# Block two's output projection done one token tile at a time, with the norms and transposes of a tile placed beside the next tile's products; the last norm by tile, too

## The reference, cut to what matters

```python
mix = jnp.concatenate([ya, yb, yc, yd], axis=-1).astype(dt)
x = x + rms_norm(mix @ w_out[l], norm_mix_post[l])
h = rms_norm(x, norm_mlp_pre[l])
ff = jnp.square(jax.nn.relu(h @ mlp_w1[l])) @ mlp_w2[l]
x = x + rms_norm(ff, norm_mlp_post[l])
```

## Time and profile before

| what | us |
|---|---|
| median of three runs (lowest, highest) | 2509.2 (2503.89, 2513.76) |
| the profiled execution: its own time | 2511.92 |
| its span in the trace | 2510.1 |
| mean granted TensorE clock over the span | 0.913 of 2.4 GHz |
| TensorE busy, share of the span | 2115.8, 84% |
| VectorE busy, share | 637.0, 25% |
| ScalarE busy, share | 325.3, 13% |

### The profile page before, as it was taken

The page is one execution under the profiler, slowest core; times in us unless marked ns, Lnnn a source line. Parts: engine busy times, 40 slices in busy tenths (PEclk is TensorE's granted clock), DMA queues, the critical chain, the costliest instruction groups (busy, mean ns, idle before and its releaser), DMA issues. The chain is left out here.

```text
span 2510.1 us, 41882 instructions
## 1 busy us (share of the span) xinstructions
PE 2115.8 (84%) x17677; PEld 1018.7 (41%) x17677; DVE 637.0 (25%) x1155; ACT 325.3 (13%) x627; POOL 253.8 (10%) x299
## 2 busy tenths in 40 slices
PE   6992469369988999999989983499988959999997
PEld 4541353324432444444334431245676324444443
DVE  2005632411211121121111213566564030000001
ACT  2002200200100111011001100143233010000000
POOL 1104500211000100100100102001210000000000
PEclk9996659579998999999999997799997979999998
DMA  9533001679999999999999999100100052211000
GB/s 369 207 128 122 3 0 34 257 307 380 397 419 419 418 418 419 410 418 418 419 419 415 418 419 358 35 34 1 47 11 35 9 201 80 88 67 75 34 0 34
DMA packets 131455, 548.47 MB, mean 219 GB/s; under 512 B 19546, under 2 KB 32878, under 8 KB 81938
## 3 DMA queue, kind: packets, MB, share of 16 engines
q1 hardware_dynamic: 105360, 506.21, 50.1%
q0 software_dynamic: 9264, 27.04, 2.8%
q10 hardware_dynamic: 16690, 13.06, 1.6%
HBM read 523.54 MB, written 22.71 MB: 218 GB/s over the span
## 5 line engine op out<-in xcount | busy, mean ns | idle before, releaser
L1250 PE MATMUL ps<-W,x_turned 128*32 128x512 f32 x3168 | 371.9, 607 | 27.3 <-DMA W<-in_w_gu 16.0
L1250 PE MATMUL ps<-W_high,x_turned 128*32 128x512 f32 x2016 | 236.4, 605 | 22.5 <-DMA W_high<-in_w_gu 16.5
L1346 DVE TENSOR_SCALAR gate<-ps 128x256 f32<-128x256 f32 x81 | 34.4, 425 | 816.7 <-PE ps L1255 816.7
L2584 PE MATMUL ps<-hT,W 128*128 128x512 f32 x512 | 224.5, 599 | 8.3 <-PEq L1450 6.3
L2622 PE MATMUL ps<-W,hid 128*128 128x512 f32 x512 | 221.6, 593 | 2.7 <-PEq L2566 1.7
L1250 PEld LDWEIGHTS ps<-W,x_turned 128*32 128x32 f32 x3168 | 97.7, 111 | 231.6 <-issue 191.7
L1268 PE MATMUL ps<-W,hidden_turned 128*32 128x256 f32 x3200 | 185.1, 384 | 2.5 <-ACT hidden_turned L1300 2.5
L2584 PEld LDWEIGHTS ps<-hT,W 128*128 128x128 f32 x512 | 97.7, 192 | 134.5 <-issue 134.5
L2622 PEld LDWEIGHTS ps<-W,hid 128*128 128x128 f32 x512 | 96.6, 190 | 127.7 <-issue 127.7
L1655 PE MATMUL ps<-hT,W 128*128 128x512 f32 x336 | 146.5, 594 | 1.7 <-PEq L1450 1.4
L1268 PEld LDWEIGHTS ps<-W,hidden_turned 128*32 128x32 f32 x3200 | 104.5, 112 | 87.4 <-issue 20.9
(11 more groups left out here) (541 smaller groups left out, 2083.2 us busy)
## 6 DMA issues: line engine op xcount, KB each, us to landing
W<-in_w_gu SPq DMA_DIRECT2D x152, 1024.0 KB
W_high<-in_w_gu SPq DMA_DIRECT2D x104, 1024.0 KB
W<-in_w_down SPq DMA_DIRECT2D x80, 1024.0 KB
W_high<-in_w_down SPq DMA_DIRECT2D x48, 1024.0 KB
W<-in_mlp_w SPq DMA_DIRECT2D x16, 2048.0 KB, 8.1
W<-in_w_ada SPq DMA_DIRECT2D x12, 2048.0 KB, 16.3
W<-in_w_in SPq DMA_DIRECT2D x10, 2048.0 KB, 16.1
moe_y<-y_rows ACTq DMA_DIRECT2D x324, 32.0 KB
```

The costliest lines, as they stand in the source:

```text
L1250: last = pe.matmul(gu_bank[SUB * j:SUB * (j + 1), :].rearrange("p (s n) -> p s n", s=2), xs[:, kk % 2, kk // 2, :], ex.view(n)[:, :, j * 2 ...
L1346: dve.tensor_scalar(gate[:], gu_bank[:, 0:256], SWIGLU_LIMIT, None, ALU.min).then_inc(gated, 1)
L2584: last = pe.matmul(ps[j % 8][:], w.tile(n)[:, kk, (j % 4) * P:(j % 4 + 1) * P], hT[:, kk, :], start=kk == 0, stop=kk == KD - 1)
```

## The change

The projection now loops over token tiles outside and column halves inside. Behind each tile's second half stand, on ScalarE and VectorE, that tile's post norm, residual add, pre norm, scaling (into `b_r` and `b_k`, memory of the mixer that is free by then, in turn) and, after its transposes, the move into `hT`. On TensorE the transposes of tile i - 1 stand behind the products of tile i. The block of `phase_norm_turn` for the MLP is gone, and so is one block end. SyncE issues the MLP's weight loads in the projection's block; the fifth and sixth go to the two slots that hold `w_out`, and wait until those are used. The banks of a tile's products are used again for its transposes. In the last phase the norm goes tile by tile too, and `out` is stored in eight pieces of 256 KB where there were four of 512 KB. Root and mean are made with one VectorE instruction fewer (the 1/D goes into the root's scale).

```diff
-class post_norm:
+class PostNorm:
...
+    def scalar(self, act, i, mm):
+        for s in range(2):
+            act.wait_ge(mm, 2 * i + s + 1)
+            act.activation(self.junk, self.k.ps[2 * i + s][:], ACT.Square, accum_out=self.ms[:, i, s:s + 1]).then_inc(self.sq, 1)
+            act.wait_ge(self.sq, 2 * i + s + 1)
+        act.wait_ge(self.summed, i + 1)
+        act.activation(self.rt[:, i:i + 1], self.rt[:, i:i + 1], ACT.Sqrt, scale=1.0 / D).then_inc(self.sd, 1)
+
+    def vector(self, dve, i):
+        dve.wait_ge(self.sq, 2 * i + 2)
+        dve.tensor_scalar(self.rt[:, i:i + 1], self.ms[:, i, 0:1], self.ms[:, i, 1:2], D * EPS, ALU.add, ALU.add).then_inc(self.summed, 1)
+        dve.wait_ge(self.sd, i + 1)
+        dve.reciprocal(self.rt[:, i:i + 1], self.rt[:, i:i + 1]).then_inc(self.vch, 1)
...
+        for s in range(2):
...
+            dve.scalar_tensor_tensor(out=self.tmp[:, s, :], in0=self.k.ps[2 * i + s][:], scalar=self.rt[:, i:i + 1], in1=self.w[:, s, :], op0=ALU.mult, op1=ALU.mult).then_inc(self.vch, 1)
+        for s in range(2):
...
+            dve.tensor_tensor(self.k.h[:, i, cols], self.k.h[:, i, cols], self.tmp[:, s, :], ALU.add).then_inc(self.done, 1)
...
+def phase_out_2(nc, k, a, w, mixT, hT, room):
...
+        @block.sync
+        def _(sp):
+            post.sync(sp)
+            w.load(sp, w.first["mlp1"], w.first["mlp1"] + SLOTS)
...
+            def turn(i):
+                for s in range(2):
+                    pe.wait_ge(xnd, 2 * i + s + 1)
+                    for q in range(4):
+                        last = pe.transpose(ps[2 * i + s][:, q * P:(q + 1) * P], xn[i % 2][:, (4 * s + q) * P:(4 * s + q + 1) * P], k.ident[:])
+                    last.then_inc(tr, 1)
+
+            for i in range(TT):
+                for half in range(2):
...
+                    for kk in range(KD):
+                        last = pe.matmul(ps[2 * i + half][:], mixT[:, kk, i * P:(i + 1) * P], w.tile(O2 + half)[:, kk, :], start=kk == 0, stop=kk == KD - 1)
+                    last.then_inc(mm, 1)
...
+                if i:
+                    turn(i - 1)
+            turn(TT - 1)
...
+        @block.vector
+        def _(dve):
+            for i in range(TT):
+                post.vector(dve, i)
+                dve.wait_ge(hsq, 2 * i + 2)
...
+                for s in range(2):
...
+                    dve.tensor_scalar(xn[i % 2][:, s * 512:(s + 1) * 512], k.h[:, i, s * 512:(s + 1) * 512], rt[:, i:i + 1], None, ALU.mult).then_inc(xnd, 1)
+                for s in range(2):
+                    dve.wait_ge(tr, 2 * i + s + 1)
...
+                    dve.tensor_tensor(hT[:, 4 * s:4 * s + 4, i * P:(i + 1) * P], ps[2 * i + s][:].rearrange("p (q t) -> p q t", q=4), gain, ALU.mult).then_inc(ev, 1)
...
@@ phase_mlp_down
-                sp.wait_ge(post.done, 2 * i + 2)
-                sp.dma_start(out[0, i * P:(i + 1) * P, :], k.h[:, i, :]).then_inc(out_done, 16)
...
+                for s in range(2):
+                    sp.wait_ge(post.done, 2 * i + s + 1)
+                    sp.dma_start(out[0, i * P:(i + 1) * P, s * 512:(s + 1) * 512], k.h[:, i, s * 512:(s + 1) * 512]).then_inc(out_done, 16)
...
@@ second_block
-            phase_norm_turn(nc, k, "_mlp", VEC["norm_mlp_pre_2"], hT, room, lambda sp: w.load(sp, w.first["mlp1"], w.first["mlp1"] + SLOTS))
```

More of the change, by code:

```diff
@@ L2492, in _, with __init__ @@
             dve.wait_ge(hfin, 2)
[L2495 to L2518, removed]
-class post_norm:
-    def __init__(self, nc, k, st, tag, wrow):
+class PostNorm:
+    def __init__(self, nc, k, st, tag, wrow, room=None):
         sem = lambda n: k.semaphore(n + tag)
@@ L2527, in __init__ @@
         self.k, self.wrow = k, wrow
[L2528 to L2532, removed]
-    def sync(self, sp):
-        sp.dma_start(self.w[:], self.wrow.rearrange("(o d) -> o d", o=1).to_broadcast([P, D])).then_inc(self.w_in, 16)
@@ L2537, in scalar @@
[L2537 to L2559, removed]
@@ new lines, in __init__ @@
+        if room is None:
+            room = sb("post_room", [P, 5, 512])[:]
+        self.w = room[:, 0:2, :]
+        self.tmp = room[:, 2:4, :]
+        self.junk = room[:, 4, :]
+        self.ms, self.rt = sb("post_ms", [P, TT, 2]), sb("post_rt", [P, TT])
+        self.w_in, self.sq, self.vch, self.summed, self.sd, self.done = (sem(n) for n in ("post_w_in", "post_sq", "post_vch", "post_sum", "post_sd", "post_done"))
+    def sync(self, sp):
+        sp.dma_start(self.w.rearrange("p a b -> p (a b)"), self.wrow.rearrange("(o d) -> o d", o=1).to_broadcast([P, D])).then_inc(self.w_in, 16)
@@ L2602, in _, with phase_mlp_down @@
                 dve.tensor_tensor(hid[:, j, :], tmp[:, j % 2, :], tmp[:, j % 2, :], ALU.mult).then_inc(sqd, 1)
-def phase_mlp_down(nc, k, a, w, hid, out):
+def phase_mlp_down(nc, k, a, w, hid, out, room):
     ps = k.ps
@@ L2610, in phase_mlp_down @@
         sem = lambda n: k.semaphore(n)
-        mm, out_done = sem("down_mm"), sem("out_done")
-        post = post_norm(nc, k, st, "_mlp", a["norm_mlp_post_2"][0])
+        mm, used, out_done = sem("down_mm"), sem("down_used"), sem("out_done")
+        post = PostNorm(nc, k, st, "_mlp", a["norm_mlp_post_2"][0], room)
         block = st.enter_context(nc.Block())
@@ L2626, in _ @@
                 if g < 7:
-                    last.then_inc(mm, 1)
-                    pe.wait_ge(mm, g + 1)
+                    last.then_inc(used, 1)
+                    pe.wait_ge(used, g + 1)
                     pe.sem_inc(w.used, 1)
@@ new lines, in _ @@
+                for s in range(2):
+                    sp.wait_ge(post.done, 2 * i + s + 1)
+                    sp.dma_start(out[0, i * P:(i + 1) * P, s * 512:(s + 1) * 512], k.h[:, i, s * 512:(s + 1) * 512]).then_inc(out_done, 16)
+            sp.wait_ge(out_done, 32 * TT)
+        @block.scalar
+        def _(act):
+            for i in range(TT):
+                post.scalar(act, i, mm)
+        @block.vector
+        def _(dve):
+            for i in range(TT):
+                post.vector(dve, i)
+            dve.wait_ge(post.done, 2 * TT)
@@ L2664, in second_block @@
             phase_mlp_up(nc, k, a, w, hT, hid)
-        phase_mlp_down(nc, k, a, w, hid, out)
+            phase_mlp_down(nc, k, a, w, hid, out, hT[:, 0:5, :])
 def build(nc, inputs):
```

77 lines of the change are left out of this document (56 added, 21 removed).

## The result

The changed kernel took 2480.75 us in the median of four runs (2477.0 to 2482.86), the kernel before beside it 2509.71 (2503.89 to 2513.76). The ratio is 0.9881, with a 95% interval of 0.9861 to 0.9901: between 25 and 35 us faster. The profiled execution has a span of 2479.2 us where before it was 2510.1.

A forecast was written before the change was run, and what follows sets the result against it. TensorE bounds the whole span but idles in two gaps, where the change can gain: 20.5 us at the projection plus 9.1 at the end, 29.6 off the 2509.2 median, gives 2479.6 us, range 2472 to 2487.

The forecast's parts named there:

- the early issues lose their cover: Gap before the MLP: if SyncE's weight issues were no longer hidden beside the products, 4.4 us would come back.
- (a): Gap after the last square: tile 2's transposes and two moves into hT keep VectorE busy until 2.3 us.
- (b): Last tile's list, from the sum to the scale: 0.98 less 0.19 for the dropped instruction, 0.79 us.
- (c): Last tile's two scales and two adds on VectorE: 0.65 three times and 0.69 for the last, ending at 5.7 us.
- (e): Last tile's pre norm: 0.79 us again to the scaling, 0.35 for its first half plus 0.1; TensorE starts at 7.7.
- (d): ScalarE's square of the second half, 0.72 us to VectorE's sum; the first half's square hidden behind the second add.
- (g): Block's end to the MLP's first instruction: 0.5 us, bringing the gap to 11.0, with SyncE no longer late.
- Beside the products: Two groups of eight transposes moved among the projection's products: 1.0 us each plus 0.1 of start, 2.2 lost.
- The end: Last square to the end of the span: 6.8 us against 15.9, a gain of 9.1 (8.7 to 9.8).
- the warm rival: Clock stays up through the gap: last transposes cost 0.8 us less, the MLP's start 2.8 less; 2476.0, chance 0.10.
- The slow rival: Tile lists on VectorE and ScalarE outlast a 13.9 us product group, stalling TensorE twice; 2519 at 25 us, chance 0.02.
- That the late weight loads hold the block's end: Before the MLP: two late loads hold the block's end and the last list isn't short; 2497, chance 0.05.

The follow-up runs named there:

- e1: Kernel before with four of the first six MLP weight loads issued in the projection's block: 2502.61 us, ratio 0.9966.
- e3: Changed kernel with all six MLP weight loads held until the projection's products are done: 2490.21 us, ratio 0.9907.
- e9: Kernel before with four MLP weight loads issued early and the changed kernel's last phase (norm by tile, eight stores): 2491.48 us, ratio 0.9931.
- e11: Changed kernel run once more with no edit, beside two others on one chip: 2480.31 us, ratio 0.9876.
- e5: Changed kernel with sixteen added VectorE instructions in the lists of token tiles 0 to 2, ahead of the scaling: 2491.19 us, ratio 0.9931.
- e6: Changed kernel with the MLP's first eight products done early, on token tiles 0 to 2, in the last tile's wait: 2473.06 us, ratio 0.9847.

## Why the prediction was right

It said 2479.6 and came out at 2480.75, inside 2472 to 2487, and the terms behind it hold one by one, save that of the clock in the MLP. By the ruler the gain is 2.3 above the 29.6 of the sum: 0.3 in the gap, 0.4 beside the products, 0.2 at the end and 1.3 in the MLP.

- **What bounds the gap.** Right, and shown by e1 and e3: the serial norms, and SyncE's issues. The prediction put the latter at 4.4 us; it measured 4.56 (e9 against the kernel before), or 4.8 in e1. Too small was its 4.4 for the case that the early issues lose their cover: with all six behind the products, e3 lost 9.6, as the short list covers less of the 20 us that they take.
- **(a) Tile 2's transposes and moves ahead of the list: 2.3.** Measured 1.93 (2012.33 to 2014.26). The new form of the move, a tensor-tensor with a repeated gain, took 0.69 and a pitch of 0.6, at the lower bound of 0.6.
- **(b) 0.79, (c) 2.6, (e) first half 0.79.** Measured 0.73, 2.60 and 0.74.
- **(d) The second square: 0.72.** Measured 0.95. The first half's square is not hidden as cleanly as assumed: with its read of the sum it runs to 0.2 behind the last add, where the second begins.
- **(e) to (g).** Scaling to transposes 0.54 (0.45), transposes and moves 2.70 (2.8), block's end 0.52 (0.5). Sum 10.71, predicted 11.0, with misses of at most 0.4 in single terms that partly cancel.
- **Beside the products: 2.2.** Measured 1.76. The second trace, e11, seems to say 0.4, but its clock stepped up earlier in the projection; against e1, where it did so too, it is 1.80. Eight transposes took 0.87 from their start to the next product, not 1.1.
- **The end: 9.1.** Measured 9.3. A store of half the size landed in 2.0, near the lower bound of 1.9 to 2.6 and not at the 2.6 that was taken. The Trainium skill, DMA: Bandwidth & Descriptors, section Anatomy of one DMA, has a fixed and a variable part, fitted for DMAs that GpSimd issues; by these, an estimate, the smaller store is 0.6 faster than the larger. Here, issued from SyncE, 2.6 became 2.0: the difference agrees, and both times stand 0.6 below the page's sums.
- **The clock.** As forecast it fell in the last tile's wait, and the MLP began at 1.2 GHz; the warm rival didn't come true here. That it left the MLP's cold start, in its words, "where it is" is the mis-sized term: against the 7.15 us of a first group at the full clock (e1) it cost 2.85 before (10.00), 1.55 in the changed kernel (8.70) and 2.6 in its second profile, e11 (9.73). And it was in the wrong place of the working: e1 and e9 (7.15 in both) show that before, too, it was no constant, but the second part of the price of SyncE's hold.

**The slow rival** (the list as the bound) is shown by e5 to act where it was said to. Its price, 2 (L - 13.9) + (L - 7.7), was too low: e5 has a third stall, 3.88 ahead of tile 2's transposes, which this leaves out. **That the late weight loads hold the block's end** didn't happen: the fifth and sixth issue were over 0.4 us behind the last square. The Trainium skill, TensorE: Matmul & The Clock Gate, Part 4, says that the full clock doesn't engage for transposes. e1 agrees with the earlier trace rows and not with the page, for these f32 transposes: between the projection and the MLP TensorE had only the 32 transposes to do, and behind them the clock was at 2.4 GHz, into the MLP.

One of the signs of being wrong tells nothing as it stands, a granted clock of 0.5 inside the projection: the changed kernel has it from 1952 to 1957, and the kernel before began its products at that level too.

The medians give 29.0 where the ruler gives 31.9. The difference is what lies ahead of the reciprocal, 1.0 later in the profiled execution of the changed kernel, and the spread of both medians. That 29.6 lies so near the first of these is in part luck.

## What to carry to other kernels

A block's end waits for every engine, the one that issues DMAs too. If a queue takes six large loads, the engine that issues them stays in the block until the last is taken, and the place of those lines in the program can be worth a good part of a new order of the computation: moving four loads gave 7.4 us where the order by tile gave 15.2, and with the last norm by tile it was half of this change's gain. Where a reduction over rows closes a phase, do it by token tile beside the next tile's products, count the room that the list has, and look at both sides of every remaining wait for products whose inputs are ready. And what is meant to be early on an in-order engine is early only if everything ahead of it in that list is.

## What the runs showed of the hardware

- SyncE's sixth 2 MB load in a row took 5.29 us to issue, in e3 as in the earlier trace rows, while the changed kernel's fifth and sixth, issued one by one 7 us apart, took 0.37 each.
- A wait of TensorE costs again when it is over. Behind 2.19 us of idle the clock was still at 2.4 GHz (e1), behind waits of 6.3 it was at 1.2 (before, changed), and the first MLP group of 6.87 us took 7.15, and 8.7 to 10.0. The length of the idle alone doesn't tell it: in the earlier trace rows the clock was at 0.50 from 2011.7, 2.3 us behind the last product, and at 1.00 until 2042, 5 us behind the last transpose. In the changed kernel 5.4 us of products in the wait kept it up (e6).
- The moment at which the clock steps up differs between profiled executions of the same products: 57.23 or 58.60 to 58.62 us in the old order, in kernels that differ elsewhere, and 60.36 and 59.03 for the changed kernel, which doesn't differ at all.
- A program of 2.5 ms repeated its last 540 us to a few hundredths in every step that the clock does not touch (changed kernel and e11), and the traces of all its variants lie up to 11.5 us apart ahead of them. A change of 1 us at the end can be read from a trace, and not from medians.
